# Ten ring slots for gathered expert rows instead of eight, in the room of a kept chunk of weights

## The reference

```python
def block(xb):                      # 128 positions, 8 heads
    q = (xb @ w_q).reshape(n, 8, 2, 128)
    s = einsum('nhie,ike->nhik', q, keys)
    top_s, top_i = top_k(s, 16)     # 16 of 128 keys, on each of two sides
    cand_s, cand_i = all 16 x 16 sums and their expert numbers
    best_s, best_pos = top_k(cand_s, 16)
    idx = take(cand_i, best_pos)    # 16 of 16384 experts a head and position
    gate = softmax(best_s)
    act = gelu(einsum('nhkd,nd->nhk', expert_u[idx], xb))
    return einsum('nhk,nhkd->nd', gate * act, expert_v[idx])
```

## Time and profile before

| | |
|---|---|
| median of three runs | 1748.86 us |
| the profiled execution's own time | 1746.73 us |
| its span, first to last instruction | 1744.9 us |
| TensorE matmuls / weight loads busy | 71% / 34% |
| VectorE / ScalarE / GpSimd busy | 68% / 28% / 35% |
| bytes moved by DMA | 665.93 MB, 382 GB/s over the span |
| chunk loads | 56 into `wbuf`, 2 into `kept` |
| gathers | 512 |
| mean granted TensorE clock | 0.838 |

### The profile page before, as it was taken

One profiled execution on the slowest core, in us unless ns is written; L12 is line 12 of the kernel. 1 busy time (PEld: TensorE's weight loads), 2 busy tenths in 40 slices (PEclk: granted clock), 3 DMA queues, 4 the chain that ended last, 5 costly groups with the idle time before them and its releaser, 6 DMA issues.

```text
span 1744.9 us, 22273 instructions
## 1 busy us (share of the span) xinstructions
PE 1236.7 (71%) x7384; PEld 598.7 (34%) x7384; DVE 1195.2 (68%) x3389; ACT 484.6 (28%) x1123; POOL 605.8 (35%) x588
## 2 busy tenths in 40 slices
PE   6865877758749978967685698796868755655654
PEld 3552222216416644422361376342226311111111
DVE  3366678665476877875746786889655777777754
ACT  0121133212213534621222244363113222222211
POOL 1032434343332323333233232422433543444452
PEclk9987998879867988989797799898989966677786
DMA  8489999999996998989999799998999999999996
GB/s 329 161 337 386 384 422 397 397 421 364 422 420 240 423 422 324 403 329 425 396 414 421 311 396 423 371 380 354 387 421 389 422 387 423 421 421 421 416 421 262
DMA packets 83781, 665.93 MB, mean 382 GB/s; under 512 B 9344, under 2 KB 9488, under 8 KB 10592
## 3 DMA queue, kind: packets, MB, share of 16 engines
q0 software_dynamic: 74464, 540.13, 76.0%
q1 hardware_dynamic: 9072, 123.98, 17.1%
q10 hardware_dynamic: 144, 0.52, 0.1%
HBM read 663.55 MB, written 1.05 MB: 381 GB/s over the span
## 4 chain that ended last, share of the span: by engine, by line
PE 32%; DMA 31%; DVE 22%; issue 8%; ACT 5%; POOL 2%; POOLq 0%; DVEq 0%; ACTq 0%; SPq 0%; PEldq 0%
DMA ring<-in_experts,idx_now 30%; PE acc L768 15%; PE act_bank L517 9%; DVE ring L1302 7%; PE dve_bank L503 3%; DVE scratch L962 2%; ACT diag L929 1%; POOL ring L445 1%; PE act_bank L702 1%; DVE scratch L1117 1%; DVE h L1323 1%; ACT L803 1%; ACT scratch L803 1%; PE act_bank L750 1%; DVE onehot L962 1%
## 5 line engine op out<-in xcount | busy, mean ns | idle before, releaser
L768 PE MATMUL acc<-ring,diag 64*64 64x512 f32 x4096 | 646.8, 763 | 343.0 <-ACT diag L929 327.5
L445 POOL DMA_INDIRECT ring<-in_experts,idx_now x512 | 578.6, 1130 | 820.0 <-PE acc L768 669.7
L1302 DVE CUSTOM_DVE_ANT_0 ring<-ring,hn 128x1024 f32<-128x1024 f32 x512 | 622.7, 1224 | 322.3 <-DMA ring<-in_experts,idx_now 292.5
L768 PEld LDWEIGHTS acc<-ring,diag 64*64 64x64 f32 x4096 | 162.3, 161 | 735.8 <-ACT diag L929 475.0
L922 ACT ACTIVATE acts<-dots 128x2 f32<-128x2 f32 x256 | 52.0, 203 | 836.4 <-DVE dots L1302 811.5
L517 PE MATMUL act_bank<-hnT,wbuf 128*128 128x128 f32 x1920 | 243.9, 287 | 22.8 <-ACT hnT L803 15.6
L517 PEld LDWEIGHTS act_bank<-hnT,wbuf 128*128 128x128 f32 x1920 | 231.7, 200 | 61.4 <-issue 61.1
L929 ACT ACTIVATE diag<-cst,coefs 128x64 f32<-128x64 f32 x512 | 150.2, 340 | 203.5 <-DVE coefs L1310 173.0
L440 POOL COPY idx_now<-idx 128x8 uint32 x64 | 21.8, 340 | 268.9 <-PE acc L768 201.8
L803 ACT ACT_TABLE_LOAD x77 | 98.8, 1283 | 11.8 <-DMA rowc<-in_rows 9.6
L1310 DVE TENSOR_TENSOR coefs<-acts,gate 128x2 f32<-128x2 f32 x256 | 41.4, 162 | 82.0 <-ACT acts L922 72.2
(11 more groups left out here) (129 smaller groups left out, 908.6 us busy)
## 6 DMA issues: line engine op xcount, KB each, us to landing
wbuf<-in_weights SPq DMA_DIRECT2D x56, 2048.0 KB
ring<-in_experts,idx_now POOLq DMA_INDIRECT x512
kept<-in_weights SPq DMA_DIRECT2D x2, 2048.0 KB, 15.0
scratch<-in_bias POOLq DMA_DIRECT2D x1, 1024.0 KB, 8.1
out<-h SPq DMA_DIRECT2D x2, 512.0 KB, 4.6
scratch<-in_bands POOLq DMA_DIRECT2D x1, 768.0 KB, 5.0
h<-in_x SPq DMA_DIRECT2D x1, 512.0 KB, 4.0
gains<-in_gains SPq DMA_DIRECT2D x1, 512.0 KB, 12.4
```

The lines of the kernel that those rows point to most:

```text
L445: pool.indirect_dma_start(ring[:, s], None, io[f"experts{layer}"], bass.IndirectOffsetOnAxis(idx_now[:, j * RING + s:j * RING + s + 1], 0) ...
L768: last[rows] = pe.matmul(acc[rows][half][home:home + HALF_P], diag[part, n % DIAGS], ring[part, n % RING, D + half * CW:D + (half + 1) * C ...
L1302: dve.tensor_tensor_reduce(out=ring[:, slot, 0:D], in0=ring[:, slot, 0:D], in1=hn[:, phase % NBLK], scale=1.0, scalar=0.0, op0=ALU.mult, o ...
```

## The change

The ring gets ten slots (10 x 2048 floats a partition). `kept` goes, whose 4096 floats a partition are what the two slots take; `idx_now` goes too. Every chunk is streamed through `wbuf`, in each block. A turn of the tables `dots`, `acts`, `coefs` stays 16 slots (BODY = TOPK), so a slot's place in the ring is now `(16 g + n) % 10`. GpSimd's loop is replaced by 512 gathers written out, each with its index column of `idx` as a constant place. The load of the gains of layer 0 moves from SP's queue to GpSimd's, behind the wait for `chunk_in1`. The gains of the two layers get a semaphore each.

```diff
-RING = 8
+RING = 10
 GROUP = 2
 DIAGS = 2 * GROUP
-BODY = 2 * RING
+BODY = TOPK
...
-        kept = sb("kept", KEEP * CH).rearrange("p (n k c) -> p n k c", n=KEEP, k=KD)
         ring = sb("ring", RING * 2 * D).rearrange("p (r d) -> p r d", r=RING)
...
-        idx_now = sb("idx_now", BODY, u32)
...
             for layer in range(DEPTH):
-                if layer:
-                    sp.wait_ge(sem("kept_free"), layer)
-                for n in range(KEEP):
-                    sp.dma_start(kept[:, n].rearrange("p k c -> p (k c)"), io["weights"][at + n]
-                                 ).then_inc(sem("kept_in"), 16)
-                if layer == 0:
-                    sp.dma_start(gains, gain_rows(0)).then_inc(sem("gain_loaded"), 16)
                 for b in range(NBLK):
-                    streamed_chunks(t, at + KEEP, CHUNKS[layer] - KEEP)
-                    t += CHUNKS[layer] - KEEP
+                    streamed_chunks(t, at, CHUNKS[layer])
+                    t += CHUNKS[layer]
...
             pool.wait_ge(sem("chunk_in1"), 16)
+            pool.dma_start(gains, gain_rows(0)).then_inc(sem("gain_loaded0"), 16)
...
-            def gather_step(layer, g):
-
-                pool.wait_ge(sem("idx_ready"), g + 1)
-                for j in range(2):
-                    for s in range(RING):
-                        if s % GROUP == 0:
-                            for rows in range(2):
-                                pool.wait_ge(sem(f"pairs_summed{rows}"), g * GROUPS + ((j * RING + s) // GROUP + 1))
-
-                        pool.sem_inc(sem("slot_opened"), 1)
-                        if s == 0:
-                            pool.tensor_copy(idx_now[:, j * RING:(j + 1) * RING],
-                                             idx[:, bass.ds(g * BODY + (j * RING - layer * NBLK * SLOTS), RING)]
-                                             ).then_inc(sem("idx_staged"), 1)
-                            pool.wait_ge(sem("idx_staged"), g * 2 + (j + 1))
-                            pool.sem_inc(sem("slot_opened"), 1)
-                        pool.indirect_dma_start(
-                            ring[:, s], None, io[f"experts{layer}"],
-                            bass.IndirectOffsetOnAxis(idx_now[:, j * RING + s:j * RING + s + 1], 0),
-                        ).then_inc(sem(f"rows_in{s}"), 16)
-
-            for layer in range(DEPTH):
-                with pool.Fori(layer * NBLK * STEPS, (layer + 1) * NBLK * STEPS) as g:
-                    gather_step(layer, g)
+            def gather(layer, n):
+
+                if n % GROUP == 0:
+                    for rows in range(2):
+                        pool.wait_ge(sem(f"pairs_summed{rows}"), n // GROUP + 1)
+                if n % TOPK == 0:
+                    pool.wait_ge(sem("idx_ready"), n // TOPK + 1)
+                at = n % (NBLK * SLOTS)
+                pool.sem_inc(sem("slot_opened"), 1)
+                pool.indirect_dma_start(
+                    ring[:, n % RING], None, io[f"experts{layer}"],
+                    bass.IndirectOffsetOnAxis(idx[:, at:at + 1], 0),
+                ).then_inc(sem(f"rows_in{n % RING}"), 16)
+
+            for n in range(PHASES * SLOTS):
+                gather(n // (NBLK * SLOTS), n)
...
-                    w = in_chunk(0, c)
+                    w = next_chunk()
...
-                    w = in_chunk(1, c)
+                    w = next_chunk()
...
             def dot(phase, g, n):
 
-                slot = n % RING
-                dve.wait_ge(sem(f"rows_in{slot}"), g * 32 + 16 * (n // RING + 1))
+                at = g * BODY + n
+                slot = at % RING
+                dve.wait_ge(sem(f"rows_in{slot}"), 16 * (at // RING + 1))
```

More of the change, by code:

```diff
@@ L40 @@
 NEG = -1.0e30
-RING = 8
+RING = 10
 GROUP = 2
 DIAGS = 2 * GROUP
-BODY = 2 * RING
+BODY = TOPK
 GROUPS = BODY // GROUP
 STEPS = SLOTS // BODY
-assert BODY == TOPK
 NWB = 2
@@ L55 @@
 CHUNKS = (L0_CHUNKS, L1_CHUNKS)
-KEEP = 1
 T_IN0 = 3
@@ L484, in chunk_used @@
                 pe.sem_inc(sem("chunks_free"), 1)
[L486 to L494, removed]
-                    chunk_used(kind)
-                elif c == KEEP - 1 and b == NBLK - 1 and layer < DEPTH - 1:
-                    pe.wait_ge(sem(kind + "_full"), jobs[kind])
-                    pe.sem_inc(sem("kept_free"), 1)
             def row_products(out, lhsT, w, first=True, last=True, cols=CW, tick=None, halfway=None):
@@ L565, in mixer0 @@
                     ins.then_inc(sem(kind + "_full"), 1)
-                    in_chunk_used(kind, 0, b, c)
+                    chunk_used(kind)
                 yield T_IN0 + 16
@@ L643, in mixer1 @@
                     ins.then_inc(sem("act_full"), 1)
-                    in_chunk_used("act", 1, b, c)
+                    chunk_used("act")
                 yield T_CB
@@ L764, in sum_pair @@
                         n = q * GROUP + odd
+                        slot = (g * BODY + n) % RING
                         for rows in range(2):
@@ L768, in sum_pair @@
                             last[rows] = pe.matmul(acc[rows][half][home:home + HALF_P], diag[part, n % DIAGS],
-                                                   ring[part, n % RING, D + half * CW:D + (half + 1) * CW],
+                                                   ring[part, slot, D + half * CW:D + (half + 1) * CW],
                                                    start=start, stop=stop, skip_group_check=True)
@@ L892, in queries @@
                 if layer == 0 and b == NBLK - 1:
-                    act.dma_start(gains, gain_rows(1)).then_inc(sem("gain_loaded"), 16)
+                    act.dma_start(gains, gain_rows(1)).then_inc(sem("gain_loaded1"), 16)
                 for hd in range(PH):
@@ L1226, in prepare @@
                 yield base
-                dve.wait_ge(sem("gain_loaded"), 16 * (layer + 1))
+                dve.wait_ge(sem(f"gain_loaded{layer}"), 16)
                 tt(hn[:, b], h[:, b], gains)
```

## The result

The changed kernel took 1704.62 us (median of four runs, 1694.48 to 1712.91) against 1748.86 (four runs, 1742.16 to 1753.86). The ratio is 0.9754, with a 95% interval of 0.9714 to 0.9794: 43 us faster, between 36 and 50. The forecast was 1718, with 1693 to 1750 as its range.

A forecast was written before the change was run, and what follows sets the result against it. DMA engines were taken as the bound, running dry in spells when VectorE is held. Ring -42.2, weights +9.9 and start +2.0 sum to -30.3 us: 1718 us from a median of 1748.86, range 1693 to 1750.

The forecast's parts named there:

- What bounds the kernel: DMA engines fill the span at about 422 GB/s, except in short deep spells when VectorE is held by other work.
- The ring, -42.2: Two more gathers under way fill idle DMA time in the spells: 42.2 us gained, bounds 15 and 70.
- The short spells' -17.4: Six short windows of low DMA rate lose 20.1 us; without 300:332, 17.4 us was counted as gained.
- each is capped at 4.97, together 29.8: Each of six long spells regains at most two gathers' DMA time, 4.97 us; together 29.8 us.
- the partly filled stretches: Stretches between the twelve windows, 550:664 the leanest, lose some 20 us in all; counted only in the 70 us bound.
- The 5 us taken off behind 524:550: No long VectorE wait for gathers follows this long spell, so 5.0 us of its filled time was not counted.
- The weights, +9.9: Streaming the kept chunk in each block adds two chunk loads, 4.19 MB at 422 GB/s: 9.9 us lost.
- The start, +2: The third chunk waits for a buffer and lands at 34.6, making TensorE late: 2 us lost, bounds 0 and 5.
- GpSimd, 0: Dropping index copies and loop gains 0, at most 6 us; loading code of written-out gathers costs at most 5 us.
- The spells' time does not come back: Rival, 0.16: nearly full consumers behind the spells leave gathers waiting in the ring; gain 15, cost 12, about 1746 us.
- Chunks land late: Rival, 0.07: deeper gather queue cuts the chunks' DMA share, TensorE waits in layer 1's projections; 1772 us.
- The change doesn't do it: Rival, 0.02: the change doesn't do what it says, only the costs stay; 1761 us.

The follow-up runs named there:

- ring8: The changed kernel with eight ring slots instead of ten: 1744.18 us, 0.9981 of the kernel before.
- kept_twice: The kernel before, with the kept chunk loaded for each block and no buffer taken away: 1753.09 us, 1.0031 of the kernel before.
- head: The changed kernel with the first block's third and fourth chunk loaded at once into idle ring slots: 1705.16 us, 0.9759 of the kernel before.
- combined: head with the next mixer beginning at slot 4 from the third phase on and layer 1's scan ending at 0.72: 1693.24 us, 0.9683 of the kernel before.
- ring6: The changed kernel with six ring slots instead of ten: 1963.76 us, 1.1249 of the kernel before.

## Why the prediction was right, point by point

**What bounds the kernel**: right. Where nothing disturbs them the DMA engines stand at 421 to 424 GB/s in both traces, and the difference of 48 us in their lost time, less the two chunks and the start, accounts for the difference in span.

**The ring, -42.2**: right in size, -40 (-48 to -32) by ring8 and the changed kernel. The short spells' -17.4 came as forecast. Wrong in part is the step "each is capped at 4.97, together 29.8": it takes the two slots as free for gathers when a spell begins. At dots 192 and 320 VectorE comes in behind, they are full, and nothing was gained (+0.2 and +2.3); at dots 128 and 160 the 16 dots around the spell gave 8.2 and 8.0, more than two gathers. So the sign named for being right, the long spells there "but some 5 us shorter each", didn't come. That the size came out is in part luck: the long spells gave 19 where 24.8 was forecast, and the partly filled stretches, put into the far bound alone ("some 20 in all"), gave some 11. An argument that would fit: behind the engines' changes of side the two slots move DMA work ahead of a spell, once for each change between DMA-bound and VectorE-bound stretches, so that two gathers for each change would be the gain wherever it appears. No run counts these changes, so this isn't shown. The 5 us taken off behind 524:550 were not borne out: that stretch lost 8.2 less (4.8 less than with eight slots).

**The weights, +9.9**: probably over-sized. kept_twice measured +5.4 (+1.0 to +9.8).

**The start, +2**: the rows, after.

```profile
13.27 9.87 PE L471 MATMUL dve_bank<-wbuf,hnT 128*128 128x512 f32 x16 [1.98 <-DMA wbuf<-in_weights]
...
34.68 8.83 PE L471 MATMUL act_bank<-wbuf,hnT 128*128 128x512 f32 x16 [4.13 <-DMA wbuf<-in_weights]
...
18.35 0.56 POOL L410 DMA_DIRECT2D gains<-in_gains  x1 [16.32 <-DMA wbuf<-in_weights]
...
100.41 1.01 POOL L428 DMA_INDIRECT ring<-in_experts,idx  x1 [77.01 <-DVEq L307]
```

And the window of the third chunk's matmuls (busy by engine, then granted clock, DMA share, GB/s):

```profile
34.68:43.50 8.82, 8.82 (x16) 3.53 (x16) 4.02 (x12) 0.00 (x0) 0.00 (x0) 0.81 0.62 241
```

The third chunk was forecast for 34.6 and begins at 34.68; GpSimd's wait, forecast at some 16, is 16.32. The fourth is there in time as forecast, but begins at 45.13 instead of 41.46, 3.7 later where 2.7 was worked out: the third one's matmuls also took 8.83 instead of 7.10. The forecast had priced the wait, but not the clock: TensorE had stood idle for 4.13 us, and of the sixteen matmuls that followed, the fifth to the eighth stand 0.85 us apart and the others 0.43 (granted clock 0.81 over all of them, where 30.16:37.30 before had 1.00), so part of the stretch ran at 1.2 instead of 2.4 GHz. The first gather is 3.2 later in this pair of traces, at 100.41. But it moves from execution to execution: nine traces with the new start (all but head and combined) have it from 97.47 to 102.42, 100.1 on average, three with the old one at 97.23, 97.95 and 99.65, 98.3 on average. That is 1.8 us, the 2 of the sum, and the sign set for being wrong, later than 102, is met by two of the nine though their start is the same program.

**GpSimd, 0**: -2.8 (-6 to 0) measured, inside the bounds; the index copies' far end of 6 was nearer than the code loading's 5.

**The sum of the rest.** Forecast +11.9, measured by ring8 -3.3 (-7 to 0). The pieces measured apart, +5.4, -2.8 and the start's 2, add up to +5. The 8 us between are about what the three intervals allow together (some 7), and no run settles whether they are real: an interaction, such as the streamed chunks falling at other places than the kept ones, stays open.

**The rivals.** "The spells' time does not come back" was half right on the mechanism and wrong on the price: it reasoned that consumers nearly full leave nothing to win, which fits the spells at dots 192 and 320, while the stretch it named and the next, dots 128 to 176, lost 29 us before and 13 after. "Chunks land late": behind the start TensorE waits for a chunk once, 0.2 us. One chunk beside gathers with the deeper ring, the queues in 333:341 of the changed kernel:

```profile
q1 hardware_dynamic: 112, 1.84, 54.0%
...
q0 software_dynamic: 213, 1.56, 46.8%
```

54% for the chunk's queue against 60%; another alignment of the same 8 us, and far from the landing of 14 us that the rival needed. "The change doesn't do it": ring8 and ring6 show that it does.

## What to carry to other kernels

Added slots of a ring between a bandwidth-bound producer and a consumer that is called away bridge a spell where they hold transfers under way when it begins; they do not shorten one into which the consumer comes already behind, with landed rows in them. Look at whether the consumer waits for the producer ahead of a spell: if it doesn't, less consumer work right there helped here, and moving it moved the spell. And compare two traces over the same piece of program, not over windows drawn by eye around each spell. The bytes that pay for the slots (0.6% more here) cost some 5 us of the 9.9 that they take at the full rate.

## What was not expected of the hardware

The depth of the ring has a steep and then a gentler side: 1964, 1744 and 1705 us for 6, 8 and 10 slots. With six, 314 us of DMA time are lost over the span, though a gather's transfer alone is 2.49 us.

The gathers of 1 MB in 8 KB rows and the 2 MB chunks together hold 421 GB/s for 290 us on end (1400:1690), with a granted TensorE clock of 0.75 in that stretch, and 423 in 544:656 with 0.92: the DMA rate doesn't follow that clock.

A gather's issue on GpSimd took 1164 ns in the changed kernel against 1130, but writing the gathers out is not the cause: the loop of kept_twice has 1149, and the written-out gathers of the other kernels lie between 1115 and 1169. Written out, they need 63 instructions fewer and 0.06 MB more of code moved.
